# Recurrent layer: the output of an earlier step stands between the next gate and its block gates

## What is computed

```python
def odd_layer(z, w_in, conv_w, conv_b, w_a, b_a, w_x, b_x, lam, w_out):
    zp = jnp.einsum('btd,de->bte', z, w_in)
    u, gate = split_cols(zp, ODD_SPLITS)
    ...
    xc = conv_b
    for tap in range(CONV_WIDTH):
        xc = xc + up[:, tap:tap + T] * conv_w[tap]
    y = (lru_direction(xc, w_a[0], b_a[0], w_x[0], b_x[0], lam[0], reverse=False)
         + lru_direction(xc, w_a[1], b_a[1], w_x[1], b_x[1], lam[1], reverse=True))
    y = y * jax.nn.silu(gate)
    return jnp.einsum('bte,ed->btd', y, w_out)
```

## Time and profile before

| | us |
|---|---|
| median of 3 runs | 1588.6 (1587.61 to 1590.26) |
| the profiled execution | 1588.83 |
| its span in the trace | 1587.0 |
| TensorE busy | 1566.6 (99%) |
| VectorE busy | 1117.7 (70%) |
| ScalarE busy | 890.7 (56%) |

### The profile page before, as it was taken

One profiled execution on the slowest core, in us unless ns is written; L12 is line 12 of the kernel. 1 busy time (PEld: TensorE's weight loads), 2 busy tenths in 40 slices (PEclk: granted clock), 3 DMA queues, 4 the chain that ended last, 5 costly groups with the idle time before them and its releaser, 6 DMA issues.

```text
span 1587.0 us, 32032 instructions
## 1 busy us (share of the span) xinstructions
PE 1566.6 (99%) x12388; PEld 1517.5 (96%) x12388; DVE 1117.7 (70%) x1718; ACT 890.7 (56%) x1402; POOL 50.9 (3%) x69
## 2 busy tenths in 40 slices
PE   8999999999999999999999999999999999999998
PEld 8888899999889999999999999999999999999997
DVE  5866676778688666688778666676567777775665
ACT  5655565597675444585646444464446755464443
POOL 0000000000001000003000000000000120000000
PEclk9999999999999999999999999999999999999998
DMA  6553224465445655554465555565654644555553
GB/s 220 156 150 104 67 79 149 154 192 173 160 133 173 199 182 183 177 173 155 140 198 167 198 181 182 185 186 184 188 183 157 198 136 146 200 175 195 182 179 116
DMA packets 74785, 264.03 MB, mean 166 GB/s; under 512 B 8592, under 2 KB 10512, under 8 KB 74704
## 3 DMA queue, kind: packets, MB, share of 16 engines
q1 hardware_dynamic: 69120, 246.76, 49.3%
q0 software_dynamic: 3824, 14.05, 2.6%
q10 hardware_dynamic: 1760, 2.09, 0.5%
HBM read 259.73 MB, written 1.05 MB: 164 GB/s over the span
## 4 chain that ended last, share of the span: by engine, by line
PE 93%; DVE 3%; ACT 2%; DMA 1%; issue 0%; ACTq 0%; SPq 0%; DVEq 0%
PE PS L1667 26%; PE PS L1669 26%; PE PS L1668 26%; PE PS L1938 3%; PE PS L2074 2%; PE PS L1869 1%; PE PS L1956 1%; PE PS L1859 1%; PE PS L1848 1%; PE PS L1845 1%; DVE w_lo L1052 1%; PE PS L1846 1%; ACT w_hi L562 1%; DMA raw<-stream 1%; PE PS L2067 0%
## 5 line engine op out<-in xcount | busy, mean ns | idle before, releaser
L1667 PE MATMUL PS<-YH,w_hi 128*128 128x256 f32 (+1 forms) x2748 | 787.6, 287 | 4.1 <-DVE YL L1067 1.6
L1669 PE MATMUL PS<-YH,w_lo 128*128 128x256 f32 (+1 forms) x2748 | 776.1, 282 | 0.0
L1668 PE MATMUL PS<-YL,w_hi 128*128 128x256 f32 (+1 forms) x2748 | 775.5, 282 | 0.0
L1052 DVE TENSOR_TENSOR w_lo<-raw,w_hi 128x1024 fp32r<-128x1024 f32 x465 | 570.9, 1231 | 120.9 <-ACT w_hi L562 117.5
L562 ACT ACTIVATE w_hi<-raw 128x1024 fp32r<-128x1024 f32 x465 | 488.8, 1053 | 110.5 <-PE PS L1669 52.2
L1667 PEld LDWEIGHTS PS<-YH,w_hi 128*128 128x128 f32 x2748 | 518.0, 188 | 10.7 <-issue 7.0
L1668 PEld LDWEIGHTS PS<-YL,w_hi 128*128 128x128 f32 x2748 | 517.0, 188 | 2.0 <-issue 0.5
L1669 PEld LDWEIGHTS PS<-YH,w_lo 128*128 128x128 f32 x2748 | 518.8, 189 | 0.0
L1668 PE MATMUL PS<-hL,w_hi 128*128 128x256 f32 x832 | 233.0, 280 | 0.0
L1669 PE MATMUL PS<-hH,w_lo 128*128 128x256 f32 x832 | 232.9, 280 | 0.0
L1667 PE MATMUL PS<-hH,w_hi 128*128 128x256 f32 x832 | 232.5, 279 | 0.0
(11 more groups left out here) (313 smaller groups left out, 1389.6 us busy)
## 6 DMA issues: line engine op xcount, KB each, us to landing
raw<-stream SPq DMA_DIRECT2D x465, 512.0 KB, 4.2
work<-stream POOLq DMA_DIRECT2D x24, 512.0 KB, 4.5
work<-work ACTq DMA_DIRECT2D x10, 136.0 KB, 4.0
X<-x SPq DMA_DIRECT2D x4, 272.0 KB, 3.4
out<-zf SPq DMA_DIRECT2D x8, 128.0 KB, 2.0
work<-work ACTq DMA_DIRECT2D x20, 34.0 KB, 2.5
work<-rope SPq DMA_DIRECT2D x1, 544.0 KB, 7.5
work<-levels POOLq DMA_DIRECT2D x1, 512.0 KB, 4.0
```

Source lines behind the costliest of these rows:

```text
L1052: dve.tensor_tensor(w_lo[:, s.slot, :], raw[:, s.slot % RAW, :], f32(w_hi[:, s.slot, :]), ALU.subtract).then_inc(lo_ready, 1)
L1667: pe.matmul(to, wh, xh, start=start, stop=False, skip_group_check=True)
L1668: pe.matmul(to, wh, xl, start=False, stop=False, skip_group_check=True)
L1669: return pe.matmul(to, wl, xh, start=False, stop=stop, skip_group_check=True)
```

## The change

`output_at(n)` gives step n the output n-6 in place of n-5, for n from 6 to 15 in place of 5 to 14. In TensorE's list the call of `output` moves from the end of a step to the place between the gate's matmuls and the block gates' wait and matmuls. `whole_order` puts the output ahead of the block gates' slab accordingly; with the shift by one step the list of slabs that comes out is the same as before. The outputs after the last step are the same, 10 to 15. VectorE's and ScalarE's lists, the ring of split slabs and the PSUM banks are unchanged.

```diff
--- before.py
+++ after.py
@@ -83,7 +83,8 @@
 
 
 def output_at(n):
-    return n - BEHIND if BEHIND <= n < STEPS - 1 else None
+
+    return n - 1 - BEHIND if BEHIND < n < STEPS else None
 
 
 def ring_order():
@@ -97,10 +98,10 @@
 
     order = []
     for n in range(STEPS):
+        if output_at(n) is not None:
+            order.append(("out", output_at(n)))
         if n % 2 == 0:
             order.append(("lru", n // 2))
-        if output_at(n) is not None:
-            order.append(("out", output_at(n)))
     return order + [("out", n) for n in range(STEPS - 1 - BEHIND, STEPS)]
 
 
@@ -1949,6 +1950,8 @@
                             pe.wait_ge(zlo_ready, DC + k + 1)
                         last = mm3(to, s, k, zH[:, k, XO:], zL[:, k, XO:], k == 0, k == DC - 1)
                     last.then_inc(w_used, 1)
+                    if output_at(n) is not None:
+                        output(output_at(n))
                     w = whole("lru", n // 2)
                     pe.wait_ge(xc_ready, n + 1)
                     for q in range(4):
@@ -1985,8 +1988,6 @@
                     gates(n)
                     for m in INPUTS_AT.get(n, ()):
                         inputs(m)
-                    if output_at(n) is not None:
-                        output(output_at(n))
                 for n in range(STEPS - 1 - BEHIND, STEPS):
                     output(n)
```

## The result

The changed kernel takes 1595.44 us (median of 7 runs, 1593.97 to 1596.91) against 1589.26 us (7 runs). The ratio is 1.0039, with a 95% interval of 1.0029 to 1.0049: 6.2 us slower, where 6.3 was forecast.

The account below looks back on a forecast made before the run. TensorE, busy for 99% of the span, was taken to bound the kernel. The order's 4.8 us plus 1.5 for the clock made 6.3 on 1588.83, 1595.1, with the median 0.2 lower: 1594.9, range 1590.8 to 1597.6.

Parts of the forecast that it names:

- The stalls: TensorE waits for bank 7 before output gates G(6), G(11), G(14), G(15): 1.04, 1.5, 1.0 and 3.6 us.
- The clock: TensorE's clock falls to half speed around the stall before gate G(15): 1.5 us, from 0 to 3.
- Rival (a): In the recurrent layer, the stalls come as forecast but TensorE's clock holds: +4.8 us, 1593.4; chance 0.32.
- Rival (d): TensorE's clock falls more than once or stays low through G(15) and O(9): 3 us more, 1598; chance 0.06.
- L(15) and the tail: Last step's block gates come 4.8 us late by the order; the layer's end moves by the same.
- The holes that go: TensorE's waits before outputs O(5), O(8) and gate G(15) vanish: 1.12 + 0.64 + 0.38 = 2.1 us saved.
- rival (b): Bank 7 is no limit in the layer, only three TensorE holes go: faster, 1586.5 us; chance 0.04.
- The other queues: Loads of WL's ring by POOL and SP's ring of gate slabs: costed at nothing.
- Rival (c): Idle ScalarE and VectorE absorb delays of G(6), G(11), G(14): within 0.2%, 3.4 us late, 1592.0; chance 0.14.
- The range: Whole kernel's time between 1590.8 and 1597.6 us, from rival (c)'s bound less a microsecond to the clock's upper bound.

Follow-up runs that it names:

- e9: The changed kernel run once more, unaltered, as partner of e10 on the same chip: 1595.57 us, ratio 1.0046 to the kernel before.
- e10: Changed kernel with eight unused matmuls of ones filling TensorE's stall before gate G(15): 1594.17 us, ratio 1.0033.
- e3: Kernel before, with output O(9) alone moved behind gate G(15): 1594.57 us, ratio 1.0034.
- e1: Changed kernel with gates spread over several PSUM banks from G(6) on: 1586.25 us, ratio 0.9983 to the kernel before.
- e4: Changed kernel with output O(9) moved back ahead of gate G(15): 1590.46 us, ratio 1.0007 to the kernel before.
- e6: Changed kernel with one VectorE scan less ahead of `gated(14)`, chunk 10 scanned in step 14: 1590.70 us, ratio 1.0011.
- e7: Changed kernel with gate G(15) alone in another PSUM bank: 1590.50 us, ratio 1.0012 to the kernel before.
- e2: Kernel before, with the same several gate banks as e1, as its control: 1588.66 us, ratio 0.9998.
- e5: Changed kernel with seven unused matmuls of ones in TensorE's stall before gate G(15): 1594.39 us, ratio 1.0034.
- e8: As e1, and in step 8 VectorE makes U(14)'s convolution ahead of chunk 4's scans: 1585.17 us, ratio 0.9977.

## Why the prediction was right

**The stalls.** Forecast from `gated`'s rows: 1.04, 1.5, 1.0 and 3.6 us before G(6), G(11), G(14) and G(15). Measured: 0.88, 1.52, 1.00 and 3.44. With the 1.07 us taken off, L(14) is 453.46 - 450.50 - 1.07 = 1.9 us late, where 1.75 was forecast. What made this possible is that the sum was not made from what is moved (8 matmuls, 3.26 us) but from when each gate's bank comes free, step by step, each delay carried to the next only where an idle time of VectorE named ScalarE.

**The clock.** Forecast 1.5 us with bounds of 0 and 3, measured 1.3, and 1.4 by e9 against e10. The prediction held the fall only a bit likelier than not; the rows of before could not decide it. That the size came out to 0.2 us is in part luck: the three profiles give 1.3, 1.5 and 2.3, by how much of G(15) ran at the lower level, and the 1.5 was taken from matmuls at the kernel's start, not worked out for G(15). Its upper bound, 2.95 for a G(15) wholly at half speed, was too large: e3 is that case and paid 2.3, since the lower level puts starts 0.21 us apart in place of 0.12, not twice as far. Rival (a), stalls without the fall, is out for the profiles taken, and the mean clocks of all executions speak against it for the rest. Rival (d), a second fall or a clock that stays low through G(15) and O(9), did not come in the changed kernel; e3 came nearest to it.

**L(15) and the tail.** L(15) was to be 4.8 us late by the order and 1.5 by the clock; it is 6.25 late, of which the order has (458.89 - 456.33 - 1.07) + (466.60 - 463.15) = 4.9 and the clock 1.3. The tail gives nothing back: from L(15) to the end of the layer it is 23.1 us both before (459.28 to 482.36) and after (466.60 to 489.69). The last scans wait for ScalarE's last roots (1.24 us idle), as said.

**The holes that go** are gone: 2.1 us, the gain of rival (b). Its error would have been to count that alone; e1 shows that with the bank out of the way it does come.

**The other queues** cost nothing: no load of WL shows among TensorE's waits in any run.

**Rival (c)**, delays absorbed before G(15), is out: the time taken off, VectorE did `gated(14)` 1.5 us later than before (458.42 - 455.86 - 1.07), where 1.39 was forecast.

**The range** was a little wider than its own terms: 1592.0 less a microsecond is 1591.0, not 1590.8, and the clock's upper bound gives 1596.4, not 1597.6. Neither matters for 1595.44.

## What to carry to other kernels

When work is moved from one place in an engine's order to another, look at what it covered where it stood, not only at the wait it is to cover in its new place: here O(9) at its old place hid a bank's release by VectorE (3.4 us), while moving O(5) and O(8) saved waits of 1.1 and 0.6. A tile that alternates between filling and draining in one bank is a hard edge between engines, and a second bank, even one borrowed from a neighbour, turned 6 us lost into 2.5 gained. A stall of TensorE can cost more than its length: here one of 3.4 us cost 1.3 us more by the clock, while three of 0.9, 1.5 and 1.0 us (e4, e6, e7), 3.4 in all, left the clock at 1.00.

## What the runs showed of the hardware

The granted clock fell to 0.50 in every profile with 3.4 to 3.8 us of standing in the midst of the kernel (changed, e9, e3), and in none whose longest stall in the layer was 1.5 us or less (before, e1, e2, e4 to e8 and e10). The price was not the same each time, 1.3, 1.5 and 2.3 us, by where the fall came: 0.4 us before G(15) started in the changed kernel, 0.4 us after in e9, and 1.4 us before in e3, where it also stayed longest, 6.8 us against 3.4 in the other two. At the lower level G(15)'s fp32r matmuls of 256 columns started 0.21 us apart, at the upper 0.12.
